# Seven block products for 14 more chunks of layer 1, with halves of 256 tokens, and the adaLN rows of layer 1 spread over four stages

## The reference

```python
D_MODEL = 1024
D_FF = -(-8 * D_MODEL // (3 * 256)) * 256
def _modulate(h, shift, scale):
    return h * (1.0 + scale) + shift
def _swiglu(h, w_gu, w_down):
    g, u = jnp.split(h @ w_gu, 2, axis=-1)
    return (jax.nn.silu(g) * u) @ w_down
```

## Time and profile before

| | us |
|---|---|
| median of 3 runs | 2304.7 (2304.56 to 2305.32) |
| profiled execution, its own time | 2303.17 |
| its span, first to last instruction | 2301.4 |
| PE busy | 2228.9 (97%) |
| PE weight loads busy | 2037.2 (89%) |
| DVE busy | 1240.4 (54%) |
| POOL busy | 1140.8 (50%) |
| ACT busy | 971.0 (42%) |

### The profile page before, as it was taken

One profiled execution on the slowest core, in us unless ns is written; L12 is line 12 of the kernel. 1 busy time (PEld: TensorE's weight loads), 2 busy tenths in 40 slices (PEclk: granted clock), 3 DMA queues, 4 the chain that ended last, 5 costly groups with the idle time before them and its releaser, 6 DMA issues.

```text
span 2301.4 us, 34267 instructions
## 1 busy us (share of the span) xinstructions
PE 2228.9 (97%) x12866; PEld 2037.2 (89%) x12866; DVE 1240.4 (54%) x2514; ACT 971.0 (42%) x1918; POOL 1140.8 (50%) x898
## 2 busy tenths in 40 slices
PE   7999999999999999999999998899999999999997
PEld 4899989989999999999998887788889899888887
DVE  6979666538731646765351555866637536112114
ACT  4232466436622751133232552256546547222223
POOL 1334455435534553456454743455545567545545
PEclk9999999999999999999999998999999999999999
DMA  7633300122124455312224454521223255333335
GB/s 270 218 117 131 101 21 27 58 78 83 58 65 152 151 168 180 110 51 88 73 88 151 149 211 166 199 94 37 65 87 97 83 193 188 119 96 101 110 117 185
DMA packets 122829, 272.45 MB, mean 118 GB/s; under 512 B 14004, under 2 KB 14260, under 8 KB 121016
## 3 DMA queue, kind: packets, MB, share of 16 engines
q1 hardware_dynamic: 112320, 244.38, 32.6%
q10 hardware_dynamic: 10360, 26.09, 3.4%
HBM read 256.77 MB, written 10.49 MB: 116 GB/s over the span
## 4 chain that ended last, share of the span: by engine, by line
PE 80%; DVE 11%; ACT 4%; DMA 2%; issue 2%; POOL 1%; ACTq 1%; SPq 0%; DVEq 0%
PE ps L2298 25%; PE ps L2310 14%; PE ps L2300 8%; PE ps L2727 7%; PE ps L2411 7%; PE ps L2905 6%; PE ps L2680 3%; PE ps L2662 3%; PE ps L2643 2%; PE ps L2487 1%; DMA raw<-in_stream 1%; POOL w_lo L711 1%; DVE pt L1907 1%; DVE max_c L1890 1%; DVE crossed L2167 1%
## 5 line engine op out<-in xcount | busy, mean ns | idle before, releaser
L711 POOL TENSOR_TENSOR w_lo<-raw,w_hi 128x512 fp32r<-128x512 f32 x608 | 825.6, 1380 | 833.5 <-ACT w_hi L789 827.6
L789 ACT ACTIVATE w_hi<-raw 128x512 fp32r<-128x512 f32 x600 | 350.4, 627 | 600.7 <-PE ps L2298 173.6
L723 POOL TENSOR_TENSOR p_sb<-p_sb,row_inv 128x768 f32<-128x768 f32 (+1 forms) x160 | 178.9, 1126 | 195.9 <-DVE row_inv L1900 194.5
L2298 PE MATMUL ps<-h_hi,w_lo 128*128 128x512 f32 (+1 forms) x672 | 251.1, 374 | 0.0
L2298 PE MATMUL ps<-h_hi,w_hi 128*128 128x512 f32 (+1 forms) x672 | 250.5, 373 | 0.0
L2298 PE MATMUL ps<-h_lo,w_hi 128*128 128x512 f32 (+1 forms) x672 | 250.5, 373 | 0.0
L2017 DVE TENSOR_TENSOR ps<-silu_g,ps 128x512 f32<-128x512 f32 (+3 forms) x52 | 36.7, 706 | 264.7 <-PE ps L2298 189.7
L2727 PE MATMUL ps<-h_hi,w_lo 128*128 128x384 f32 (+1 forms) x408 | 146.7, 360 | 0.7 <-ACT gates_a L1138 0.7
L2727 PE MATMUL ps<-h_lo,w_hi 128*128 128x384 f32 (+1 forms) x408 | 144.1, 353 | 0.0
L2727 PE MATMUL ps<-h_hi,w_hi 128*128 128x384 f32 (+1 forms) x408 | 144.0, 353 | 0.0
L2298 PEld LDWEIGHTS ps<-h_hi,w_hi 128*128 128x128 f32 x672 | 126.1, 188 | 18.6
(11 more groups left out here) (283 smaller groups left out, 5895.7 us busy)
## 6 DMA issues: line engine op xcount, KB each, us to landing
raw<-in_stream SPq DMA_DIRECT2D x648, 256.0 KB, 3.0
ada_raw_tokens_a<-in_w_ada SPq DMA_DIRECT2D x31, 512.0 KB, 5.2
ada_raw_merge_c<-in_w_ada SPq DMA_DIRECT2D x31, 512.0 KB, 4.3
ada_raw_gate_up<-in_w_ada SPq DMA_DIRECT2D x18, 512.0 KB, 3.5
bias_sb<-in_bias ACTq DMA_DIRECT2D x32, 256.0 KB, 2.8
scratch<-xr ACTq DMA_DIRECT2D x16, 512.0 KB, 4.8
xr<-scratch SPq DMA_DIRECT2D x14, 512.0 KB, 4.9
first_raw<-in_w_first SPq DMA_DIRECT2D x5, 1024.0 KB, 14.5
```

The lines of the kernel that those rows point to most:

```text
L711: nc.gpsimd.tensor_tensor(w_lo[:, u % 2, cols], raw[:, u % 2, cols], w_hi[:, u % 2, cols].bitcast(F32), ALU.subtract).then_inc(S("lo_made" ...
L723: nc.gpsimd.tensor_tensor(p, p, row_inv[:, c:c + 1].broadcast_to([P, keys]), ALU.mult).then_inc(S("p_ready"), 1)
L789: nc.scalar.activation(w_hi[:, s, cols], raw[:, s, cols], ACT.Copy).then_inc(S("hi_made"), 1)
L2298: last = nc.tensor.matmul(bank(0), tile, x[:, k, 0:split], start=start, stop=stop)
```

## The change

Seven products are now used in parts 1 and 2 of layer 1's gate_up as well (6 + 8 chunks), with halves of 256 tokens (`half = ph.width // 2`). The crossing, its hi copies and rests run in part 0 of down of layer 1 too; in both layers the hi copies are spread (`CROSSED_BESIDE`) and the rests follow them. The adaLN units of layer 1 move: tokens_a 15 to 9, merge_c 15 to 9, part 0 of down of layer 0 from 6 to 10 (now in steps 0 to 3), and 8 in part 0 of gate_up of layer 1. Two waits are new: SP's for `unit_done` in a bridge behind a sevenfold part, and PE's for `hidden_lo` there.

```diff
-ADA_WINDOWS = {("tokens_a", 0): (16, 32), ("merge_c", 0): (32, 48), ("tokens_a", 1): (66, 81), ("merge_c", 1): (81, 96)}
+ADA_WINDOWS = {("tokens_a", 0): (16, 32), ("merge_c", 0): (32, 48), ("tokens_a", 1): (70, 79), ("merge_c", 1): (79, 88)}
 ADA_LOADS = {("tokens_a", 0): {2: 3, 3: 3, 4: 3, 5: 3, 6: 3, 7: 1}, ("merge_c", 0): {3: 3, 7: 2, 8: 3, 9: 2, 10: 3, 11: 3},
-             ("tokens_a", 1): {2: 3, 3: 3, 4: 3, 5: 3, 6: 3}, ("merge_c", 1): {3: 3, 7: 2, 8: 3, 9: 2, 10: 3, 11: 2}}
-ADA_AFTER_PAIR = ((4, 6, 6, 0), (4, 6, 5, 0))
+             ("tokens_a", 1): {2: 3, 5: 3, 6: 3}, ("merge_c", 1): {3: 3, 8: 3, 11: 3}}
+ADA_AFTER_PAIR = ((4, 6, 6, 0), (3, 3, 3, 0))
 ADA_BOTH = 64
 
-ADA_BESIDE = {("gate_up", 0): (48, 4), ("down", 0): (60, 2)}
-ADA_BESIDE_END = 66
+ADA_BESIDE = {(0, "gate_up", 0): (48, 60), (0, "down", 0): (60, 70), (1, "gate_up", 0): (88, 96)}
+ADA_BESIDE_END = (70, 96)
...
+CROSSED_BESIDE = {3: ((0, 1), 5), 4: ((2,), 8), 5: ((3,), 10)}
...
-    return ph.kind == "gate_up" and ph.tiles == ALLT and ph.part > 0
+    return ph.kind == "gate_up" and ph.part > 0 and (ph.layer > 0 or ph.tiles == ALLT)
...
-    return ADA_BESIDE.get((ph.kind, ph.part)) if ph.layer == 0 and ph.tiles == ALLT and ph.kind in ("gate_up", "down") else None
+    return ADA_BESIDE.get((ph.layer, ph.kind, ph.part))
+
+
+def ada_batch(ph, n):
+
+    first, end = ada_beside(ph)
+    return min(first + ADA_SLOTS * n, end), min(first + ADA_SLOTS * (n + 1), end)
...
                     sp.wait_ge(S("merged"), at(ph, "merged"))
+                    if sevenfold(after(ph, -1)):
+                        sp.wait_ge(S("unit_done"), ph.unit)
                     if at(ph, "shifted"):
                         sp.wait_ge(S("shifted"), at(ph, "shifted"))
                         sp.wait_ge(S("stored"), at(ph, "stored"))
-                    if ph.layer == 0 and ph.part == 1:
-                        sp.wait_ge(S("ada_used"), PRIME - ADA_FIRST + ADA_BESIDE_END)
+                    if ph.part == 1:
+                        sp.wait_ge(S("ada_used"), PRIME - ADA_FIRST + ADA_BESIDE_END[ph.layer])
...
-                first, count = ada_beside(ph)
-                n, rest = divmod(u - ph.unit - 2, 2)
-                if rest or n not in range(count):
+                n, rest = divmod(u - ph.unit - 2, 1 if ph.kind == "down" else 2)
+                if rest or n < 0:
                     return
-                if first == ADA_UNITS and n == 0:
+                first, end = ada_batch(ph, n)
+                if first == end:
+                    return
...
-                load_ada("gate_up", first + ADA_SLOTS * n, ADA_SLOTS)
+                load_ada("gate_up", first, end - first)
...
+            def crossed_his(ph, some, steps):
+
+                half = ph.width // 2
+                act.wait_ge(S("crossed"), CROSS_STEPS * ph.layer + steps)
+                act.wait_ge(S("ada_used"), PRIME - ADA_FIRST + ADA_BESIDE_END[ph.layer])
+                for x in some:
+                    nc.scalar.activation(crossed_hi[x][:, :, 0:half], crossed[x][:, :, 0:half], ACT.Copy).then_inc(S("crossed_hi"), 1)
...
-                    a, c, d, b = (ps[:, seven_bank(n) + x, 0:HALF] for x in range(4))
+                    half = ph.width // 2
+                    a, c, d, b = (ps[:, seven_bank(n) + x, 0:half] for x in range(4))
+                    u2, p1 = pair_u2[:, 0:half], pair_p1[:, 0:half]
...
+                        if unrolled and beside:
+                            ada_units("gate_up", *ada_batch(ph, n))
...
-                    if n == KD - 3 and steps:
-                        ada_biased(ADA_UNITS, ADA_BOTH, MODS_READY[1, 0])
-                        for x in range(4):
-                            crossed_rest(x)
-                    if n == KD - 2:
+                    if n == 4 and steps:
+                        if not ph.layer:
+                            ada_biased(ADA_UNITS, ADA_BOTH, MODS_READY[1, 0])
+                        crossed_rest(ph, 0)
+                        crossed_rest(ph, 1)
+                    if n == 5 and steps:
+                        crossed_rest(ph, 2)
+                    if n == 6:
                         first_sums_of(nxt, 0)
+                        if steps:
+                            crossed_rest(ph, 3)
...
+                if sevenfold(after(ph, -1)):
+                    pe.wait_ge(S("hidden_lo"), at(ph, "hidden_lo") - 1)
...
-                            last = nc.tensor.matmul(ps[:, bank, 0:HALF], half_slot(w, slot)[:, k * P:(k + 1) * P], x[:, first + k, a:a + HALF],
+                            last = nc.tensor.matmul(ps[:, bank, 0:half], half_slot(w, slot)[:, k * P:(k + 1) * P], x[:, first + k, a:a + half],
```

More of the change, by code:

```diff
@@ L1341, in seven_products @@
             def seven_products(ph):
-                last = SEVEN * ph.chunks
+                last, half = SEVEN * ph.chunks, ph.width // 2
                 for j in range(last):
@@ L1355, in seven_products @@
                     else:
-                        slot, half = divmod(j + 4 - last, 2)
-                        act.wait_ge(raw_ready[slot][half], 8 * (ph.unit + ph.units) + 16)
-                        nc.scalar.activation(half_slot(w_hi, 2 * slot + half), half_slot(raw, 2 * slot + half), ACT.Copy).then_inc(S("hi_made"), 1)
+                        slot, rest = divmod(j + 4 - last, 2)
+                        act.wait_ge(raw_ready[slot][rest], 8 * (ph.unit + ph.units) + 16)
+                        nc.scalar.activation(half_slot(w_hi, 2 * slot + rest), half_slot(raw, 2 * slot + rest), ACT.Copy).then_inc(S("hi_made"), 1)
                     if i == 6:
@@ L1396, in down @@
                                 factor_split(nxt, 2 * (n - KD + 2) + j)
[L1397 to L1398 removed]
+                        if ph.part == 0 and n in CROSSED_BESIDE:
+                            crossed_his(ph, *CROSSED_BESIDE[n])
                     return
@@ L2004, in attention, with chunk_of_hidden @@
                 fold_low(count - 1)
-            def chunk_of_hidden(ph, n, c, count, a, b, bank, wide, gate=silu_g):
+            def chunk_of_hidden(ph, n, c, count, a, b, bank, wide, gate=silu_g, half=None):
                 w = b - a
@@ L2185, in gate_up @@
                 beside = ada_beside(ph)
-                if beside and beside[0] == ADA_UNITS:
-                    dve.wait_ge(S("cond_loaded"), 16 * 5)
+                if beside:
+                    dve.wait_ge(S("cond_loaded"), 16 * (8 if ph.layer else 5))
                 def pair(i, ada):
@@ L2193, in pair @@
                         if ada:
-                            ada_three("gate_up", beside[0] // ADA_SLOTS + n)
+                            ada_units("gate_up", *ada_batch(ph, n))
                         dve.wait_ge(S("unit_done"), ph.unit + 4 * i + 2 * c + 2)
                         chunk_of_hidden(ph, ph.first + n, c, n, 0, w, chunk_bank(ph, c) + 2, w > LAT)
-                loaded = beside[1] // 2 if beside else 0
+                loaded = ph.chunks // 2 if beside else 0
                 for i in range(loaded):
                     pair(i, True)
+                if beside and ph.layer:
+                    ada_biased(*beside, MODS_GATE)
                 if loaded < ph.chunks // 2:
@@ L2211, in several @@
                         n = DOWN_BANKS * i + s
-                        if unrolled and s % 2 and beside and n // 2 < beside[1]:
-                            ada_three("gate_up", (beside[0] + ADA_SLOTS * (n // 2)) // ADA_SLOTS)
+                        if unrolled and beside:
+                            ada_units("gate_up", *ada_batch(ph, n))
                         dve.wait_ge(S("unit_done"), ph.unit + n + 1)
@@ L2896, in seven_products @@
                         if n == 0 and ph.part == 1:
-                            pe.wait_ge(S("crossed_lo"), CROSSED[i] + 1)
+                            pe.wait_ge(S("crossed_lo"), 4 * ph.layer + CROSSED[i] + 1)
                     else:
-                        x_hi, x_lo, first, a = h_hi, h_lo, KD // 2 * (i > 0), HALF * (i == 6)
+                        x_hi, x_lo, first, a = h_hi, h_lo, KD // 2 * (i > 0), half * (i == 6)
                     wait_for(pe, factor_lo(ph, j))
```

45 lines of the change are left out of this document (22 added, 23 removed).

## The result

The changed kernel takes 2308.66 us (median of 20 runs, 2304.73 to 2312.12); the kernel before, over 20 runs, 2304.63 us. The ratio is 1.0015, with an interval from 1.0008 to 1.0022: 0.15% slower, inside the 0.2% that the prediction took for no change, and 0.7 us from the forecast of 2308. Its profiled execution took 2311.64 us (span 2309.8), 3 us above the median, so the two profiled executions stand 8.5 us apart where the medians stand 4 apart.

What follows compares the result with a forecast made beforehand. PE's work and its few waits bound the kernel; layer 1's seven products would be bound by the last-sum loop. From 2303.2 us, +23.5 + 3 + 0 - 11.4 - 9.1 - 2.4 gave 2306.8, median 2308; range 2288 to 2327.

Steps and rivals of the forecast that it cites:

- The loop: Layer 1 gate_up parts 1 and 2: last sum, weight loads, next first sum, splits, hidden part; 13.2 us a turn.
- The bound of 11.1: Lower bound of a turn in layer 1's seven products, if only POOL and its sums count; upper bound 14.0 us.
- The lock of the sums: DVE sums with two SBUF inputs and POOL's w_lo exclude each other over a common port pair for the whole instruction.
- the 11.6 us: Layer 1 chunk cost if no sum runs beside a w_lo: 7 x 1.27 + 4 x 0.68 us.
- The first two chunks of a part: Layer 1 gate_up parts 1 and 2: first chunk 10.1 us, weights already there; second about 11.8, partly covered.
- +23.5: Layer 1 gate_up parts 1 and 2 together: 74.7 us for 65.3 and 101.1 for 87.0; range +9 to +33.
- Rows: Moved adaLN loads remove PE stalls in layer 1: tokens_a gains 11.4 us (8 to 13), merge_c 9.1 (5 to 9.5).
- the third batch: Layer 1 tokens_a: the last adaLN loads still delay raw one unit later, so 1.5 us of PE wait remain.
- Gate_up part 0: Layer 1: eight more adaLN operations meet a mostly waiting DVE, 4 MB of loads in 87 us; cost 0 (to 2).
- Ends: After the last chunk of layer 1's parts: +0.5 us before down, +2.5 at the bridge, together +3, range 0 to 5.
- The rival of a lower clock: Layer 1 parts 1 and 2: clock falls in PE's new gaps, a turn some 15 us, total 2328 us; chance 0.12.
- a granted clock below 0.9 in these parts: Layer 1 gate_up parts 1 and 2: listed among the signs that would show the forecast wrong.

Runs made afterwards that it cites:

- two edits: Against the changed kernel: last sum moved ahead of the hidden part, 2297.3 us; POOL's w_lo cut to 256 of 512 columns, 2294.4 us; both, 2275.6 us.

## Why the prediction was right

**The loop** (13.2 us a turn): right in mechanism, place and size; 13.3 was measured. The way from the first sum to the end of the last, 7.64 us in layer 0 less 1.0 for the columns, became 7.5 because the last sum is disturbed by 0.9 in nearly every turn, which is why the prediction went toward its upper end. What it did not say is that a second loop stood close behind, its last load released 0.25 us before it was wanted; the prediction does not suffer from that, but who had read it as advice and shortened the first loop by 3 us would have got 1.1. The bound of 11.1 (POOL and its sums alone) was too low to be of use.

**The lock of the sums.** The one sum that suffers is the last, 0.9 us in nearly every turn; the other three keep 0.68 to 0.69. With 256 columns for POOL it takes 0.68 to 0.77 in twelve of fourteen chunks. So the trace and the runs agree with the Trainium skill (SBUF — State Buffer, section SBUF: two separate sides) that the two exclude each other, but the 11.6 us that the rule gave as a sum over all of them was not what bound.

**The first two chunks of a part**: 10.1 + 11.8 = 21.9 forecast, 22.2 (10.1 + 12.2) and 23.1 (10.6 + 12.5) measured on PE. The chunks behind them take PE 13.4 us each on average, 0.2 more than forecast, ten times. Together that makes +26.7 for +23.5, the largest error among the terms that were worked out.

**Rows.** tokens_a brought 13.2 for 11.4: the 1.5 us that I kept for the third batch did not come. I had mis-sized PE's work in hand: it begins a new half unit every 4.3 us there (1385.97, 1390.29, 1394.61), 8.6 us a unit where I had 5.4, so that the w_lo behind the third batch, ready at 1395.67, is not wanted before 1398.9. merge_c 9.4 for 9.1, down 2.5 for 2.4. The 0 to 2.4 that the four more adaLN operations might take back in down did not show: the stage has the same length in the kernel with six of them there (517.1 us from norm rows to norm rows) and with ten (517.3).

**Gate_up part 0** was costed at 0 (to 2) and took 0.6 to 4.4. The step that failed is the sentence that takes 4 MB over 87 us as a mean. It leaves out the condition, 1 MB more, and all 5 MB are issued within the 22 us from 1938.6, the first 2.5 MB in one burst ahead of weights.

**Ends.** The last bridge took +2.4 for +2.5, with PE's waits for hid_lo and acc; down part 1 took +0.3 for +0.5. The second ln_rows and raw loads went as the text said, behind unit_done.

**The clock.** The rival of a lower clock came to little, though the clock fell: 0.87 in the window from 2070 above, 0.95 as a mean of part 2. One of the prediction's signs of being wrong, a granted clock below 0.9 in these parts, is thus there in single windows of 13 us and not in the mean. In the turns it cost nothing: the way from the first sum to the end of the last takes 7.5 us in every one, at either clock, because PE is not in it. Only behind the last turn is there no loop to hide it: the last chunk of part 1, with 0.84 in 2097 to 2108, took PE 14.3 us, that of part 2, at 1.00, 12.1.

The errors in the profiled execution add up: +3.2 in the products, +4.4 in part 0 and +1.5 in the bridge against -2.2 in the rows and the down of layer 0, -0.3 in the ends and -2.0 at the start, and it ran 5 us over the 2306.8 of the sum. The median came 3 us under that execution. So 2308.66 against 2308 is partly luck, closer than the terms deserve: errors of both signs cancel, and two of them (part 0, the start) are of those that move from execution to execution.

## What to carry over

A form that saves multiplications pays only if every other loop in a turn is shorter than the engine's new turn: walk from one buffer's release through load, helper engines and back to the release, in a stage that already runs that form, and scale only what scales. Look for the second-longest loop before shortening the first: two edits that bring 11 and 14 us alone brought 33 together. When loads are moved into a stage with room, compare their burst, not their mean, with the lead of the loads behind them. And measure the parts of a change singly: here the moved rows alone bring 24 us, and the seven products, the part with the saving in multiplications, cost 25.

## What was not expected of the hardware

A sum of 128x512 with both inputs in SBUF took 1.55 to 1.60 us in place of 0.69 when POOL had a row of four w_lo in work, in nearly every turn, and in the same position: the order of the two engines locks in with the loop. With POOL's operations at half their width the same sum took 0.68 to 0.77 in most turns. Which of the two engines pays turned on 0.1 us: in down of layer 0 it was DVE in one kernel (2.82 us for 1.75) and POOL in another (2.78 for 1.60).

The length of a gap did not tell by itself what the clock did: it stayed at 1.00 through one of 2.4 us and was 0.66 in the five us after one of 2.5 us, the same as after one of 3.6 us.

Four loads of 256 KB with nothing else on the queue needed 5.4 to 6.1 us, once 6.8, from the end of the last sum, which lets the first of them be issued, until the first sum that waits for all of them started, but 3.3 to 3.6 us from the last issue when the other three had gone ahead.
